# Two fused transformer layers in split fp32: weight slots re-laid so that the two SBUF operands of a matmul sit 192 bytes apart modulo 256

## The chip, the cores and the metric

The kernel runs on one core of a Trainium2 chip. The metric is the device time of one execution in microseconds (us); lower is better. Before the change three runs gave a median of 1536.1 us (1534.24 to 1539.58).

## The reference, cut to what matters

Two layers are computed one after the other on 256 tokens with a model width of 2048, all in fp32. What costs time is the product of a small activation matrix with large weight matrices, each weight used once:

```python
# layer 1 (mLSTM + pooling)
h = rmsnorm(x, norm_pre_w)                      # 256 x 2048
q, k, v, o, z, i, f, u, zb, ga, gb = split(h @ w_in)
y_a = sigmoid(o) * mlstm(silu(conv(q,k)), v, i, f) * silu(z)
y_b = (pool(u) @ pool_w) * pool_scale * silu(zb)
merged = sigmoid(ga) * (y_a @ w_proj_mlstm) + sigmoid(gb) * (y_b @ w_proj_pool)
x = x + rmsnorm(merged @ w_out, norm_post_w)
# layer 2 (16 meta tokens in front: 272 tokens), differential + latent attention
h = rmsnorm(concat(meta, x), attn_norm_w)
a_q, a_k, a_v, a_g, b_cq, b_ckv, b_kr, b_g = split(h @ w_in_2)
s = where(rel >= 0, qk_scores, -inf)            # causal mask in both attentions
oA, oB = diff_attention(...), mla_attention(rmsnorm(b_cq) @ w_uq, rmsnorm(b_ckv) @ w_ukv, b_kr)
y = rmsnorm(x + concat(oA * silu(a_g), oB * silu(b_g)) @ w_out_2, final_norm_w)
```

## The kernel before, in words

**Split products.** Every weight product runs as three fp32r matmuls: high part of the weights times high part of the activations, high times low, low times high. The weights come as a stream of 474 slots. A slot is 256 rows of one 512-column block: two chunks of 128 rows (`c` = 0, 1), each 128 partitions x 512 columns of 4 bytes.

**The ring.** SyncE loads slot n into `raw[n % 4]` (512 KB). ScalarE's `split` (L783) copies it to `wh[n % 4]`, rounded to fp32r; VectorE's `split` (L1077) writes the rest to `wl[n % 4]`. Both work LEAD = 3 slots ahead of TensorE and wait for `slots_done` or for each other, so a slot is split while TensorE works on an earlier one. The `wh` and `wl` buffers are 4096 bytes each per partition, one behind the other, and the two chunks of a slot are 2048 bytes apart.

**The matmuls.** `pe_group` issues all of them, in two forms:

- By feature (L298, L300, L302): the weights are the stationary operand, 128 columns of a chunk at a time (LDWEIGHTS), and the activations of the same 128 rows are the moving operand, 256 columns (272 where the meta tokens are included). A chunk gives 4 blocks x 3 = 12 matmuls, a slot 24.
- By token (L288 to L290): the activations are stationary (128 tokens) and the weights move, 512 columns. A slot gives 12 matmuls. Stages V and WO, the group cq, the second half of UKV, and W2.

**The stages**, in order, with their moving or stationary activations: QK (X), V (X, by token), OZ (X, with the mLSTM heads' small matmuls between slots), UZ (X), MG (groups ga and gb on X, pa on Y, pb on Z), WO (by token), then layer 2: CKQ, AK, AV, AQ on X2, UQ and UKV on the latent activations, G on X2 with attention's small matmuls between slots, W2 (by token).

**Where the operands lie.** In X, Y, Z and the latents `cqh`, `cql` a 128-row chunk of activations is 1024 bytes per partition and starts at a multiple of 256 from the common base. X2 (`x2h`, `x2l`) has 272 columns, so its chunk kc starts 1088*kc bytes in, which is 64*kc modulo 256; where a stage takes the 256 real tokens alone (AQ, G, cq) it starts another 64 bytes later. The weights' blocks start at multiples of 256 bytes everywhere, because 512 columns, 128 columns and the slot are all multiples of 256 bytes. Below, the offset of a matmul is the address of its moving operand less that of its stationary operand, modulo 256, both in bytes within a partition. Before the change it is 0 in all matmuls by feature on X, Y, Z and the latents. In AQ and G it is 64*(kc+1) modulo 256: chunks 0, 4, 8, 12 have 64, chunks 1, 5, 9, 13 have 128, chunks 2, 6, 10, 14 have 192 and chunks 3, 7, 11, 15 have 0. In AK and AV it is 64*kc.

**The mask.** In the attention quarters of G, VectorE adds `cmask` (0 or -1e30) to the latent attention's scores (L1286). The other attention uses `rel` (key position less query position, or -1e30 where masked). Both tables, 416 columns each, are part of `const`, loaded once at the start.

## Time and profile before

| | us |
|---|---|
| median of three runs | 1536.1 |
| the profiled execution, its own time | 1533.42 |
| its span, first to last instruction | 1531.6 |
| TensorE matmul busy (with modelled ends) | 1489.3 |
| TensorE weight load busy | 1407.8 |
| VectorE busy | 839.1 |
| ScalarE busy | 711.0 |
| mean granted TensorE clock | 0.994 |

The records of matmuls overlap: each shows 0.28 us although the next starts 0.12 us later. The pace is therefore read from the start of one to the start of the next, or from the number of instructions in a long window, and never from the mean duration.

### The profile page before, as it was taken

The page shows a single profiled execution, that of the slowest core. Times are in us where ns is not written, and L with a number is a line of the kernel's source. Part 1 is how long each engine was busy: PE and PEld are TensorE (multiplying, and loading weights), DVE is VectorE, ACT ScalarE, POOL GpSimd, SP SyncE. Part 2 cuts the span into 40 slices and gives each one's busy share as a digit, 9 for nine tenths or more (in the row PEclk, how much of TensorE's full clock was granted, in tenths as well). Part 3 has the DMA queues.
Part 4 walks back from the last instruction along what each step waited for, and adds up shares of the span by engine and source line. Part 5 has one row for each costly group of instructions (what it writes and reads, how often), then busy time and mean ns, then how long its engine had stood idle before and what let it go on. Part 6 is the DMA issues. An engine that isn't in the chain of part 4 may idle for free.

```text
span 1531.6 us, 27814 instructions
## 1 busy us (share of the span) xinstructions
PE 1489.3 (97%) x10848; PEld 1407.8 (92%) x10848; DVE 839.1 (55%) x1032; ACT 711.0 (46%) x931; POOL 65.8 (4%) x90
## 2 busy tenths in 40 slices
PE   6999999999999999999999999979999999999997
PEld 6999998899999999999999998868999997888886
DVE  5667664546646555545454544556444444556754
ACT  5454445445455433334333434445433344666542
POOL 0000000101000000000000000000000001111000
PEclk9999999999999999999999999999999999999999
DMA  7565555654455556666566566646655553333563
GB/s 266 168 203 170 177 175 179 196 162 155 160 151 184 173 164 169 186 183 180 178 187 183 176 192 231 212 124 225 202 158 173 166 157 106 102 105 111 195 215 126
DMA packets 70647, 265.01 MB, mean 173 GB/s; under 512 B 7841, under 2 KB 7841, under 8 KB 69281
## 3 DMA queue, kind: packets, MB, share of 16 engines
q1 hardware_dynamic: 69552, 254.45, 53.9%
q0 software_dynamic: 1024, 9.57, 1.7%
q8 instruction: 51, 0.84, 0.2%
q14 instruction: 20, 0.16, 0.0%
HBM read 259.79 MB, written 4.19 MB: 172 GB/s over the span
## 4 chain that ended last, share of the span: by engine, by line
PE 93%; DVE 2%; ACT 2%; DMA 1%; issue 1%; DVEq 0%; POOL 0%; ACTq 0%; SPq 0%; POOLq 0%
PE ps L298 23%; PE ps L302 23%; PE ps L300 23%; PE ps L288 5%; PE ps L289 5%; PE ps L290 5%; PE ps L397 2%; DMA metan<-in_meta 1%; PE ps L635 1%; PE ps L469 1%; PE ps L477 1%; PE ps L642 1%; DVE wl L1077 1%; DMA xn<-in_x 0%; PE ps L640 0%
## 5 line engine op out<-in xcount | busy, mean ns | idle before, releaser
L1077 DVE TENSOR_TENSOR wl<-raw,wh 128x1024 fp32r<-128x1024 f32 x474 | 580.0, 1227 | 570.1 <-ACT wh L783 562.5
L783 ACT ACTIVATE wh<-raw 128x1024 fp32r<-128x1024 f32 x474 | 499.0, 1059 | 563.5 <-PE ps L302 440.5
L298 PE MATMUL ps<-xh,wh 128*128 128x256 f32 x1792 | 510.9, 285 | 1.8 <-DVE xl L1091 1.8
L302 PE MATMUL ps<-xh,wl 128*128 128x256 f32 x1792 | 507.7, 283 | 0.0
L300 PE MATMUL ps<-xl,wh 128*128 128x256 f32 x1792 | 507.6, 283 | 0.0
L298 PEld LDWEIGHTS ps<-xh,wh 128*128 128x128 f32 x1792 | 344.4, 192 | 2.3 <-DVE xl L1091 2.0
L300 PEld LDWEIGHTS ps<-xl,wh 128*128 128x128 f32 x1792 | 344.5, 192 | 0.3
L302 PEld LDWEIGHTS ps<-xh,wl 128*128 128x128 f32 x1792 | 344.5, 192 | 0.0
L298 PE MATMUL ps<-x2h,wh 128*128 128x256 f32 (+1 forms) x688 | 198.8, 289 | 3.5 <-ACTq L896 3.3
L302 PE MATMUL ps<-x2h,wl 128*128 128x256 f32 (+1 forms) x688 | 195.2, 284 | 0.0
L300 PE MATMUL ps<-x2l,wh 128*128 128x256 f32 (+1 forms) x688 | 195.1, 284 | 0.0
L298 PEld LDWEIGHTS ps<-x2h,wh 128*128 128x128 f32 x688 | 129.6, 188 | 7.8 <-issue 6.9
L300 PEld LDWEIGHTS ps<-x2l,wh 128*128 128x128 f32 x688 | 129.7, 188 | 0.1
L302 PEld LDWEIGHTS ps<-x2h,wl 128*128 128x128 f32 x688 | 129.4, 188 | 0.0
L298 PE MATMUL ps<-yh,wh 128*128 128x256 f32 x256 | 72.4, 283 | 0.0
L300 PE MATMUL ps<-yl,wh 128*128 128x256 f32 x256 | 72.4, 283 | 0.0
L302 PE MATMUL ps<-yh,wl 128*128 128x256 f32 x256 | 72.4, 283 | 0.0
L1120 DVE SCALAR_TENSOR_TENSOR work<-ps,small,work 128x255 f32<-128x255 f32 (+2 forms) x96 | 39.5, 475 | 23.6 <-ACT work L824 23.5
L288 PE MATMUL ps<-wh,mh 128*128 128x512 f32 x128 | 50.0, 391 | 2.4 <-DVE wl L1077 2.4
L288 PE MATMUL ps<-wh,oh 128*128 128x512 f32 x128 | 50.3, 393 | 1.8 <-DVE ol L1390 1.8
L289 PE MATMUL ps<-wl,oh 128*128 128x512 f32 x128 | 49.8, 389 | 0.0
L290 PE MATMUL ps<-wh,ol 128*128 128x512 f32 x128 | 49.8, 389 | 0.0
(321 smaller groups left out, 1781.1 us busy)
## 6 DMA issues: line engine op xcount, KB each, us to landing
raw<-in_w_stream SPq DMA_DIRECT2D x474, 512.0 KB, 3.7
xn<-in_x SPq DMA_DIRECT2D x2, 1024.0 KB, 6.1
xr<-in_x POOLq DMA_DIRECT2D x1, 2048.0 KB, 15.1
x_kept<-xr POOLq DMA_DIRECT2D x1, 2048.0 KB, 9.8
x1r<-x_kept POOLq DMA_DIRECT2D x1, 2048.0 KB, 10.4
out<-yn SPq DMA_DIRECT2D x4, 512.0 KB, 2.7
const<-in_const SPq DMA_DIRECT2D x1, 1044.0 KB, 12.5
poolw<-in_pool_w POOLq DMA_DIRECT2D x1, 1024.0 KB, 5.4
```

What stands on the lines that cost most here:

```text
L288: pe.matmul(o, hi[:, kc, t], wh[r][:, c, 0:cols], start=a, stop=False)
L289: pe.matmul(o, hi[:, kc, t], wl[r][:, c, 0:cols], start=False, stop=False)
L290: last = pe.matmul(o, lo[:, kc, t], wh[r][:, c, 0:cols], start=False, stop=z)
L298: pe.matmul(out_at(j), wh[r][:, c, f], hi[:, kc, tokens], start=st, stop=False, skip_group_check=True)
L300: pe.matmul(out_at(j), wh[r][:, c, f], lo[:, kc, tokens], start=False, stop=False, skip_group_check=True)
L302: last = pe.matmul(out_at(j), wl[r][:, c, f], hi[:, kc, tokens], start=False, stop=z, skip_group_check=True)
L397: return pe.transpose(o, i, ident[0:n, 0:n])
L469: last = pe.matmul(ps[:, 5, st * S:st * S + w], kst[:, dt, st * P:(st + 1) * P], qk[:, bass.ds(h * 2 + dt, 1), st * P:S].rearrange("p o s ...
L477: last = pe.matmul(ps[:, 6 + t, 0:VW], lhs, vn[:, st, bass.ds(h * VW, VW)], start=st == 0, stop=st == t)
L783: act.activation(wh[r][:, :, :], raw[r][:, :, :], ACT.Copy).then_inc(wh_done, 1)
L1077: tt(wl[r][:, :, :], raw[r][:, :, :], wh[r][:, :, :].bitcast(F32), ALU.subtract).then_inc(split_done, 1)
L1120: last = stt(out=work[0][:, jj, sh:S], in0=banks(j)[:, jj, 0:S - sh], scalar=small[:, bass.ds(SMALL["conv_w"][0] + q * 16 + 4 * jj + 3 - s ...
```

## The change

The slots `wh` and `wl` grow from 4096 to 4352 bytes (1088 columns), a multiple of 256, and inside a slot the first chunk's start and the distance between the two chunks depend on what the slot is used for. `slot_view` gives the two chunks; the two splits write through it and `pe_group` reads through it.

| layout | first column | pitch | for | offset after |
|---|---|---|---|---|
| BY_FEATURE | 16 (64 bytes) | 512 | all by-feature groups on X, Y, Z, latents | 192 |
| BY_TOKEN | 0 | 512 | v, wo, uv, w2 | 0, as before |
| SECOND | 0 | 528 | aq, g | 64 in even slots, 192 in odd slots |
| SECOND_KEYS | 16 | 528 | cq, ckv, ak, av | by feature 192 in even slots, 64 in odd; cq 0 and 128 |

The last column is worked out from the addresses: a slot's two chunks are kc = 2k and 2k+1, X2 moves on by 64 bytes per chunk, and so does a slot with a pitch of 528 columns; what is left changes by 128 from slot to slot. The first three slots of V and of WO keep the layout of the stage before.

The buffers behind the ring move up by 2048 bytes, a multiple of 256. To make room, `cmask` goes from `const` (1044 KB to 836 KB), and the masked scores come from `rel`: `min(rel + 1e29, scores)`, one SCALAR_TENSOR_TENSOR in place of one TENSOR_TENSOR of the same 416 columns.

No instruction is added, removed or moved on any engine. Some of the splits become 128 x 2 x 512 in place of 128 x 1024.

```diff
+SLOT_W = 1088
+BY_FEATURE, BY_TOKEN, SECOND, SECOND_KEYS = (16, 512), (0, 512), (0, 528), (16, 528)
+LAYOUT_OF = {"v": BY_TOKEN, "wo": BY_TOKEN, "uv": BY_TOKEN, "w2": BY_TOKEN, "cq": SECOND_KEYS, "ckv": SECOND_KEYS,
+             "ak": SECOND_KEYS, "av": SECOND_KEYS, "aq": SECOND, "g": SECOND}
+def slot_layouts():
+    out = []
+    for name, kinds, times in STAGES:
+        of = [LAYOUT_OF.get(kind, BY_FEATURE) for kind in kinds for _ in range(slots_of(kind))] * times
+        if name in ("V", "WO"):
+            of[:LEAD] = out[-LEAD:]
+        out += of
+    return out
-    ("ones", 128), ("dmask", 384), ("inv", 64), ("rel", KEYS), ("cmask", KEYS),
+    ("ones", 128), ("dmask", 384), ("inv", 64), ("rel", KEYS),
-    R_X, R_C, R_Y, R_Z, R_V, R_T = 49152, 83968, 116736, 149504, 165888, 182336
+    R_X, R_C, R_Y, R_Z, R_V, R_T = 51200, 86016, 118784, 151552, 167936, 184384
-    wh = [sb(f"wh{r}", [P, SLOT_KC, COLS], F32R, (RING + r) * KB4) for r in range(RING)]
-    wl = [sb(f"wl{r}", [P, SLOT_KC, COLS], F32R, (2 * RING + r) * KB4) for r in range(RING)]
+    wh_at = [sb(f"wh{r}", [P, SLOT_W], F32R, RING * KB4 + r * 4 * SLOT_W) for r in range(RING)]
+    wl_at = [sb(f"wl{r}", [P, SLOT_W], F32R, RING * KB4 + (RING + r) * 4 * SLOT_W) for r in range(RING)]
+    def slot_view(slot, layout):
+        first, pitch = layout
+        return slot[:, first:first + SLOT_KC * pitch].rearrange("p (c n) -> p c n", n=pitch)[:, :, 0:COLS]
...
-                        pe.matmul(out_at(j), wh[r][:, c, f], hi[:, kc, tokens], start=st, stop=False,
+                        pe.matmul(out_at(j), whr[:, c, f], hi[:, kc, tokens], start=st, stop=False,
...
-            act.activation(wh[r][:, :, :], raw[r][:, :, :], ACT.Copy).then_inc(wh_done, 1)
+            act.activation(slot_view(wh_at[r], layout), raw[r][:, :, :], ACT.Copy).then_inc(wh_done, 1)
...
-                    tt(pm[odd][:, :], ps[:, 4, 0:KEYS], cn("cmask"), ALU.add)
+                    stt(out=pm[odd][:, :], in0=cn("rel"), scalar=1e29, in1=ps[:, 4, 0:KEYS], op0=ALU.add,
+                        op1=ALU.min)
```

## Rows read from the trace of the kernel before

**Rows 1.** The page: busy shares, and the chain that ended last.
```profile
PE 1489.3 (97%) x10848; PEld 1407.8 (92%) x10848; DVE 839.1 (55%) x1032; ACT 711.0 (46%) x931; POOL 65.8 (4%) x90
...
PE 93%; DVE 2%; ACT 2%; DMA 1%; issue 1%; DVEq 0%; POOL 0%; ACTq 0%; SPq 0%; POOLq 0%
```

**Rows 2.** Stretch 620:900 (MG), line L298 alone: busy and count.
```profile
620.00:900.00 280.00, 220.09 (x779) 149.34 (x778) 1.00 0.61 182
```

**Rows 3.** Timeline, AQ's second group, chunks 8 to 11 (start us, us).
```profile
1221.70 0.28 PE L298 MATMUL ps<-x2h,wh 128*128 128x256 f32 x1
...
1223.12 0.28 PE L298 MATMUL ps<-x2h,wh 128*128 128x256 f32 x1
...
1224.55 0.28 PE L298 MATMUL ps<-x2h,wh 128*128 128x256 f32 x1
...
1225.14 0.28 PE L302 MATMUL ps<-x2h,wl 128*128 128x256 f32 x1
...
1225.82 0.28 PE L302 MATMUL ps<-x2h,wl 128*128 128x256 f32 x1
1225.93 0.28 PE L298 MATMUL ps<-x2h,wh 128*128 128x256 f32 x1
...
1226.87 0.28 PE L302 MATMUL ps<-x2h,wl 128*128 128x256 f32 x1
...
1227.35 0.28 PE L298 MATMUL ps<-x2h,wh 128*128 128x256 f32 x1
```

**Rows 4.** Timeline, G's third group, chunk 6: entered after attention's matmuls.
```profile
1368.11 0.28 PE L300 MATMUL ps<-x2l,wh 128*128 128x256 f32 x1
...
1369.28 0.28 PE L302 MATMUL ps<-x2h,wl 128*128 128x256 f32 x1
```

**Rows 5.** Timeline, cq (by token on X2): two rows nine matmuls apart.
```profile
1043.75 0.39 PE L289 MATMUL ps<-wl,x2h 128*128 128x512 f32 x1
...
1045.82 0.39 PE L289 MATMUL ps<-wl,x2h 128*128 128x512 f32 x1
```

**Rows 6.** Stretch 214:254.8 (V, 15 slots), line L288 alone: busy and count.
```profile
214.00:254.80 40.80, 23.34 (x60) 11.26 (x60) 1.00 0.62 182
```

**Rows 7.** Lines by shape: busy us, mean ns, idle before and what ended it.
```profile
L298 PE MATMUL ps<-xh,wh 128*128 128x256 f32 x1792 | 510.9, 285 | 1.8 <-DVE xl L1091 1.8
...
L783 ACT ACTIVATE wh<-raw 128x1024 fp32r<-128x1024 f32 x474 | 499.0, 1059 | 563.5 <-PE ps L302 440.5 <-PE ps L290 108.6 <-issue 9.6
...
L1077 DVE TENSOR_TENSOR wl<-raw,wh 128x1024 fp32r<-128x1024 f32 x474 | 580.0, 1227 | 570.1 <-ACT wh L783 562.5 <-issue 4.0
...
L1253 DVE SCALAR_TENSOR_TENSOR sbd<-const,ps 128x416 f32<-128x416 f32 x16 | 9.7, 645 | 19.9 <-PE ps L635 19.9
...
L1286 DVE TENSOR_TENSOR pm<-ps,const 128x416 f32<-128x416 f32 x8 | 4.7, 584 | 0.0
```

**Rows 8.** Timeline, AK's second group: the starts of chunks 8, 10, 11, 12.
```profile
1120.44 0.28 PE L298 MATMUL ps<-x2h,wh 128*128 128x272 f32 x1
...
1123.46 0.29 PE L298 MATMUL ps<-x2h,wh 128*128 128x272 f32 x1
...
1124.98 0.28 PE L298 MATMUL ps<-x2h,wh 128*128 128x272 f32 x1
...
1126.46 0.28 PE L298 MATMUL ps<-x2h,wh 128*128 128x272 f32 x1
```

**Rows 9.** VectorE's lines in stretch 71.4:117.4 (QK, 16 slots).
```profile
L1077 DVE TENSOR_TENSOR wl<-raw,wh 128x1024 fp32r<-128x1024 f32 x17 | 20.7, 1225 | 8.8 <-ACT wh L783 7.7 <-issue 0.9
L1120 DVE SCALAR_TENSOR_TENSOR work<-ps,small,work 128x254 f32<-128x254 f32 (+2 forms) x24 | 9.9, 474 | 6.1 <-ACT work L824 6.1
L1130 DVE TENSOR_TENSOR qk<-work,work 128x1024 f32 x2 | 2.4, 1220 | 0.0
```

**Rows 10.** Timeline, OZ's first head: `pt` made and taken.
```profile
304.31 0.55 DVE L1435 SCALAR_TENSOR_TENSOR pt<-ps,dmat 128x384 f32<-128x384 f32 x1
...
307.57 1.47 PE L477 MATMUL ps<-vn,pt 128*128 x6
```

More of the change, by code:

```diff
@@ L69 @@
 GATE_W = 32 + H
+SLOT_W = 1088
[10 more added lines that the diff above has]
+    return out
+LAYOUTS = slot_layouts()
 OUT_ORDER = (0, 2, 1, 3)
@@ L254, in pe_group @@
     def pe_group(pe, n, frees, out_at, moving, tiles, tokens, ring=0, kcs=KC, cols=COLS, before=None,
-                 chunk=lambda kc: kc, first_tile_early=False):
+                 chunk=lambda kc: kc, first_tile_early=False, like=None):
         hi, lo = moving
@@ L271, in pe_group @@
             r = (ring + k) % RING
+            layout = LAYOUTS[(n if like is None else like) + k]
+            whr, wlr = slot_view(wh_at[r], layout), slot_view(wl_at[r], layout)
             def free(c, at):
@@ L287, in pe_group @@
                         free(c, m)
-                        pe.matmul(o, hi[:, kc, t], wh[r][:, c, 0:cols], start=a, stop=False)
-                        pe.matmul(o, hi[:, kc, t], wl[r][:, c, 0:cols], start=False, stop=False)
-                        last = pe.matmul(o, lo[:, kc, t], wh[r][:, c, 0:cols], start=False, stop=z)
+                        pe.matmul(o, hi[:, kc, t], whr[:, c, 0:cols], start=a, stop=False)
+                        pe.matmul(o, hi[:, kc, t], wlr[:, c, 0:cols], start=False, stop=False)
+                        last = pe.matmul(o, lo[:, kc, t], whr[:, c, 0:cols], start=False, stop=z)
                 else:
@@ L297, in pe_group @@
                         free(c, j)
-                        pe.matmul(out_at(j), wh[r][:, c, f], hi[:, kc, tokens], start=st, stop=False,
+                        pe.matmul(out_at(j), whr[:, c, f], hi[:, kc, tokens], start=st, stop=False,
                                   skip_group_check=True)
-                        pe.matmul(out_at(j), wh[r][:, c, f], lo[:, kc, tokens], start=False, stop=False,
+                        pe.matmul(out_at(j), whr[:, c, f], lo[:, kc, tokens], start=False, stop=False,
                                   skip_group_check=True)
-                        last = pe.matmul(out_at(j), wl[r][:, c, f], hi[:, kc, tokens], start=False, stop=z,
+                        last = pe.matmul(out_at(j), wlr[:, c, f], hi[:, kc, tokens], start=False, stop=z,
                                          skip_group_check=True)
@@ L418, in groups @@
             in_loop = not isinstance(i, int)
+            one = 1 if in_loop else i
             for j, kind in enumerate(kinds):
@@ L424, in groups @@
                          [slice(m * P, (m + 1) * P) for m in range(TOK)] if by_token else None, slice(0, S),
-                         kcs=slots_of(kind) * SLOT_KC,
+                         kcs=slots_of(kind) * SLOT_KC, like=FIRST[name] + one * per + off,
                          first_tile_early=name == "WO" and not in_loop and (i, j) == (1, 1), before=before and (lambda k, j=j, kind=kind: before(j, kind, k)))
@@ L753, in body @@
                         if not isinstance(i, int) or here + k + LEAD < end:
-                            split(here + k + LEAD, (n0 + off + k + LEAD) % RING)
+                            like = n0 + (i if isinstance(i, int) else 1) * per + off + k + LEAD
+                            split(here + k + LEAD, (n0 + off + k + LEAD) % RING, LAYOUTS[like])
                         if late:
@@ L788, in _ @@
             act.activation(xsq[:, m, :], xn[:, m, :], ACT.Square, accum_out=stat[:, m:m + 1]).then_inc(s_x_squares, 1)
-        split(0, 0)
+        split(0, 0, LAYOUTS[0])
         def high_parts(hi, b, name, s):
@@ L802, in _ @@
             if b + 1 < LEAD:
-                split(b + 1, b + 1)
+                split(b + 1, b + 1, LAYOUTS[b + 1])
         def out_squares(q, m):
@@ L1040, in between @@
             act.drain().then_inc(s_out_squares, 1)
-            split(n, n % RING)
-            split(n + 1, (n + 1) % RING)
+            split(n, n % RING, LAYOUTS[n])
+            split(n + 1, (n + 1) % RING, LAYOUTS[n + 1])
             x1_squares(2)
             x1_squares(3)
-            split(n + 2, (n + 2) % RING)
+            split(n + 2, (n + 2) % RING, LAYOUTS[n + 2])
             for b in range(4):
@@ L1084, in _ @@
                 ts(xn[:, m, q], xn[:, m, q], stat[:, 2 + m:3 + m], None, ALU.mult).then_inc(s_x_normed, 1)
-        split(0, 0)
+        split(0, 0, LAYOUTS[0])
         def low_parts(lo, hi, b, name, s):
@@ L1098, in _ @@
             if b + 1 < LEAD:
-                split(b + 1, b + 1)
+                split(b + 1, b + 1, LAYOUTS[b + 1])
         def split_high_low(hi, lo, src, s):
@@ L1498, in between @@
             x1_rows(1)
-            split(n, n % RING)
+            split(n, n % RING, LAYOUTS[n])
             x1_scale(1)
-            split(n + 1, (n + 1) % RING)
-            split(n + 2, (n + 2) % RING)
+            split(n + 1, (n + 1) % RING, LAYOUTS[n + 1])
+            split(n + 2, (n + 2) % RING, LAYOUTS[n + 2])
             dve.tensor_copy(x2h[:, :, 0:META], metat[:, :, :])
@@ L1695, in const_array @@
     rel = np.where(kpos <= pos, kpos - pos, far)
-    mask = np.where(kpos <= pos, 0.0, far)
     put("rel", np.concatenate([rel[:P, :K0], rel[P:, :]], 1))
-    put("cmask", np.concatenate([mask[:P, :K0], mask[P:, :]], 1))
     slopes = np.exp2(-np.arange(1, 9, dtype=np.float32)) * 8.0
```

9 lines of the change are left out of this document (5 added, 4 removed).

## The prediction

> **What bounds the kernel.** I read the busy shares first: TensorE is busy 97% of the span, and the chain that ended last is TensorE for 93% of it [rows 1]. ScalarE and VectorE are at 46% and 55%, and each waits: ScalarE's split stood idle for 563.5 us in total, 549.1 of it ended by TensorE's matmuls, and VectorE's waited for ScalarE's [rows 7]. So weights are not late; TensorE's own pace sets the time, and what counts is the time from one matmul's start to the next.
>
> The second view is the count of matmuls in a long quiet stretch. In 280 us of MG there are 779 records of L298 [rows 2], which takes every third place; one hangs over the window's left edge, so 280 us / (3 x 778) = 120.0 ns each, with the clock granted in full. At 2.4 GHz, the upper level, 256 columns alone would be 106.7 ns, so 13.3 ns, or 32 cycles, of each are something else. All of these have offset 0.
>
> The third view is the timeline of AQ, because there the same form of matmul, 256 moving columns and 128 x 128 weights, runs at four offsets in turn. Its rows begin at 1221.70, where the ninth chunk (kc = 8) starts. From chunk start to chunk start, 12 matmuls each [rows 3]:
>
> - kc = 8, offset 64: 1.42 us, 118.3 ns each
> - kc = 9, offset 128: 1.43 us, 119.2 ns
> - kc = 10, offset 192: 1.38 us, 115.0 ns
> - kc = 11, offset 0: 1.42 us, 118.3 ns
>
> The first few of a chunk are a passage from the offset before. Inside chunk 10, from 1225.14 to 1225.82, six matmuls take 0.68 us: 113.3 ns each [rows 3], or 272 cycles against the 288 of offset 0. That is the pattern that the change can give to most of the kernel. The last four of chunk 11, back at offset 0, take 0.48 us: 120.0 each, X's own pace. But 113.3 is not the only pattern at offset 192. Chunk 6 of G's third group, also at 192, was entered after attention's matmuls; its second matmul starts at 1368.11 and its twelfth at 1369.28 [rows 4], ten steps in 1.17 us, 117 ns each to within the timeline's rounding of 1 ns; I use 117.8, where chunk 8's 118.3, passage and all, also points. So there are two patterns at 192, and which one a run falls into hangs on how it is entered. I went through all 24 chunks of AQ and G at this offset in the timeline: 16 settle at 113.3, 8 stay near 117.8 to their end. Of the 7 chunks entered straight from the chunk before, 6 settle at 113.3; of the 17 entered after other work, 10. None changes pattern once it has settled, and none is slower than 120.
>
> Is it the relation of the two addresses, or the moving operand's own address? In V and in cq the moving operand is the same `wh` and `wl` at the same addresses, and only the stationary side moves. V gives 60 records of one line in three over 40.8 us, 226.7 ns each [rows 6]; in cq nine steps take 2.07 us, 230.0 ns each [rows 5]. The stationary side matters too, so own address alone is refuted; the relation is the simpler reading.
>
> The Trainium skill speaks against the change: "TensorE: Matmul & The Clock Gate", Part 2, says that the weight load reads through a port of its own and takes no SBUF bandwidth from the running matmul, and its "Back-to-back issue gap" gives N/2.4 + 2.5 = 109.2 ns for 256 columns. By that every offset would run alike and the change be worth nothing; were 109.2 reached instead, an estimate from that page is 72 us of gain. The trace agrees with neither: 113.3 and 120.0 stand in one program for the same form.
>
> **The change part by part.**
>
> *By-feature matmuls on X, Y, Z and the latents.* They go from offset 0 to 192. They are the slots of QK 64, OZ 64, UZ 32, MG 112 and UQ 6: 278 x 24 = 6672, of which 1792 x 3 on X [rows 7]. The first slot ran in the start's half-clock time and some fifty steps hold a wait or other work, so 6630 steps count. At 113.3 in place of 120.0 each saves 6.67 ns, 44.2 us in all; at 117.8 it saves 2.2 ns, 14.6 us. These are the two ends. They divide by runs without a break: QK (64 slots, one run after the start) is worth 10.0 or 3.3 us; from the last pooling matmul of UZ through MG (113 slots, 2700 steps) 18.0 or 6.0; the rest of UZ, two runs, 5.1 or 1.7; OZ (64 slots), broken 24 times by the heads' matmuls, 10.2 or 3.4, and with 10 of 17 such entries in the fast pattern about 7.5; UQ 1.0 or 0.3. I take the fast pattern for the long runs, since the straight entries favour it and long sections let a passage settle: 10.0 + 18.0 + 5.1 + 7.5 + 0.8 = 41.4 us.
>
> *AQ and G, 48 slots, 1152 matmuls.* Only the odd slots get 192, the even ones stay at 64. Before, the four offsets average (118.3 + 119.2 + 115.0 + 118.3)/4 = 117.7. After, half stays at 117.8 and half comes to between 113.3 and 117.8, with two thirds fast 114.8. Gain 576 x 2.9 = 1.7 us, less 0.1. I take 1.6.
>
> *AK, AV and ckv, 32 x 24 + 16 x 9 = 912 matmuls of 272 columns.* Chunks 8 and 9 (offsets 0 and 64) take 3.02 us together, chunk 10 (128) 1.52 and chunk 11 (192) 1.48 [rows 8], so 125.8, 125.8, 126.7, 123.3 ns. Half at 192 and half at 64 afterwards is 124.6 on average against 125.4: 0.7 us.
>
> *By token.* V, WO, uv and W2 keep offset 0. Three slots each of V and WO, 72 matmuls, get offset 64; by cq's 230.0 that is 72 x 3.3 = 0.2 us lost. cq itself, 96 matmuls, has half at 0 afterwards: 48 x 3.3 = 0.2 won. Nil together, and within 0.7 either way.
>
> *The splits.* The same columns, some as two pieces of 512. Neither row shows such a shape; nearest are 1059 ns and 1227 ns themselves [rows 7]. I take no change, and bound it by none and by a tenth more, 0.23 us per slot for the pair. Both are hidden while TensorE takes 2.72 us per slot: V already runs there, 12 x 226.7 ns, without a break over 15 slots [rows 6]. The tightest place is QK, where VectorE also does the convolution: 20.7 + 9.9 + 2.4 = 33.0 us in 46 [rows 9], 72%; TensorE at 113.3 ns does these 16 slots in 43.5 us, and VectorE is at 76%. VectorE still idles 8.8 + 6.1 us there. The group's burst of convolution work, four or five slots long, loses at most 5 x 0.16 = 0.8 us of its lead. I take 0, up to 1 us lost.
>
> *The heads.* TensorE reaches `pt` at 307.57, 2.7 us after VectorE made it (304.31 + 0.55) [rows 10]. Three or four slots between question and answer shrink by 0.16 us each, 0.64 at most. No new wait.
>
> *The mask.* TENSOR_TENSOR of 416 columns is 584 ns, a SCALAR_TENSOR_TENSOR with the same table and PSUM is 645 [rows 7]: 8 x 61 ns = 0.5 us on VectorE, beside TensorE's slot work. 0. The shorter `const` is loaded behind the first four slots and nothing waits for it: 0.
>
> Sum: 41.4 + 1.6 + 0.7 + 0 = 43.7 us, less 0.7 for small waits and the rounding of entries: 43. The profiled execution's 1533.4 becomes 1490.4 (its span 1531.6 to 1488.6). The median of the runs lies 2.7 us above the profiled one, so the forecast in its terms is 1493.
>
> **The rivals.**
>
> A. *One of the long runs locks into the slow pattern.* For: 8 of 24 chunks did, mostly those entered after other work, and both long runs begin so. Against: straight entries settled fast. Price: MG's run 18.0 - 6.0 = 12 us, 1505; QK's 6.7 us, 1500; both 1512; every run slow is 14.6 + 1 or so of gain, 1520.
>
> B. *The address relation is not what sets the pace of X.* AQ and G differ from X in the operands' region and pitch too, and weight load and moving operand may not meet there at all; the other 13.3 ns would be a fixed cost. Then nothing changes but the small terms: 1534 to 1537. For: only X2's chunks show 113.3. Against: offset-0 chunks of X2 run at X's 120.0 once settled [rows 3], and V against cq.
>
> C. *Slower: at a fixed offset of 192 X settles in a third, worse pattern.* For: taking the stationary side off offset 0 did make cq slower, by 3.3 ns a matmul [rows 5, 6]. If each of the 6630 steps lost the same 3.3 ns to the 120.0, they would cost 22 us: 1558. It decides as soon as the settled step is above 120.0 ns. Against: no chunk at 192 shows it, 24 of them.
>
> **How the numbers follow.** Main case 1493 (1487 to 1498): 0.52. Rival A, 1498 to 1521: 0.31. B: 0.09. C: 0.05. A gain over 49 us, if a long run finds a pattern still faster than any seen: 0.03. The range of 1487 to 1519 holds the main case and nearly all of A, 0.82; the main case's own range is 1487 to 1498. A change under 0.3%, 4.6 us, can't be told from none. Faster: 0.52 + 0.31 + 0.03 = 0.86, and a little of B goes either way, 0.01 of it faster; same 0.07; slower 0.06.
>
> **What would show it.** Right: 280 us of MG hold some 824 records of L298 in place of 779; the timeline in MG steps by 0.11 and 0.12 us, 0.34 for three; V and W2 still 12 matmuls in 2.72 us; ScalarE's split still released by TensorE, with less idle. A shows as steps of 117.8 ns through all of MG or QK; OZ may show both between heads. B shows 120.0 in MG with 113.3 still in G's odd slots. New waits of TensorE for `wl` in QK would show the cover gone. The forecast is wrong if the settled step on X is neither 113.3 nor 117.8 ns.

## The result, and the profile after

The changed kernel takes 1517.8 us (median of 4 runs, 1516.8 to 1520.2) against 1535.3 for the kernel before (1534.2 to 1539.6): ratio 0.988, 95% interval 0.986 to 0.991. That is 17.4 us of gain where 43 were forecast. The time lies inside the range, and beside the figure of rival A for "every run slow", 1520. The profiled execution took 1517.3, its span 1515.5.

The page of the changed kernel, its busy shares, its chain, and the costliest lines (line, engine, operation, count, busy us and mean ns, idle before and what ended it). By-feature matmuls are now L323, L325 and L327.

```profile
PE 1471.6 (97%) x10848; PEld 1389.7 (92%) x10848; DVE 839.0 (55%) x1032; ACT 711.2 (47%) x931; POOL 66.5 (4%) x90
...
PE 93%; DVE 2%; ACT 2%; DMA 2%; issue 1%; DVEq 0%; POOL 0%; ACTq 0%; SPq 0%; POOLq 0%
...
L1104 DVE TENSOR_TENSOR wl<-raw,wh 128x1024 fp32r<-128x1024 f32 x474 | 579.9, 1227 | 555.5 <-ACT wh L810 547.8
L810 ACT ACTIVATE wh<-raw 128x1024 fp32r<-128x1024 f32 x474 | 499.3, 1059 | 545.7 <-PE ps L327 422.4
L323 PE MATMUL ps<-xh,wh 128*128 128x256 f32 x1792 | 506.6, 283 | 2.3 <-DVE xl L1119 2.3
```

What bounds the kernel is what bounded it before [rows 1]: TensorE is busy 97%, and only its total shrank, 1489.3 to 1471.6. The splits take 1227 and 1059 ns as before [rows 7], and TensorE waits for no new thing. The idle of ScalarE's split fell from 563.5 to 545.7 us, about what TensorE's total lost.

Line L323 alone in two quiet stretches, QK and MG: length, busy and count of matmuls and of weight loads, granted clock, DMA share, GB/s.

```profile
30.00:190.00 160.00, 127.24 (x453) 84.96 (x454) 1.00 0.60 187
620.00:900.00 280.00, 222.71 (x793) 148.72 (x793) 1.00 0.62 186
```

The second row answers to [rows 2], the records of L298 in the same stretch before: 793 records in place of 779, where the forecast wanted 824. 280 / (3 x 792) = 117.8 ns a step; QK's 160 / (3 x 452) = 118.0 says the same to the rounding of a count. The timeline, one slot of MG, rows nine steps apart (start us, us):

```profile
699.85 0.28 PE L323 MATMUL ps<-xh,wh 128*128 128x256 f32 x1
...
700.91 0.28 PE L323 MATMUL ps<-xh,wh 128*128 128x256 f32 x1
```

1.06 us over nine steps is 117.8. In OZ both patterns stand in one stage. First eight steps of a slot from before a head's work, then nine of one behind it:

```profile
298.29 0.28 PE L325 MATMUL ps<-xl,wh 128*128 128x256 f32 x1
...
299.20 0.28 PE L323 MATMUL ps<-xh,wh 128*128 128x256 f32 x1
...
307.85 0.28 PE L325 MATMUL ps<-xl,wh 128*128 128x256 f32 x1
...
308.91 0.28 PE L325 MATMUL ps<-xl,wh 128*128 128x256 f32 x1
```

0.91 / 8 = 114 ns, within the timeline's rounding of 113.3; 1.06 / 9 = 117.8. Stage by stage, from the first matmul of a stage to the first of the next (W2 to the end of the span), with the mean step, from one matmul's start to the next one's, over all steps without other work or a wait between. "In the fast pattern" are slots that settle at 113.3 ns:

| stage | us before | after | gain | step before | after | slots in the fast pattern |
|---|---|---|---|---|---|---|
| QK | 192.4 | 189.0 | 3.4 | 120.0 | 117.8 | 0 of 64 |
| OZ | 213.0 | 208.6 | 4.3 | 119.9 | 117.0 | 13 of 64 |
| UZ | 99.1 | 95.9 | 3.2 | 120.0 | 115.8 | 14 of 32 |
| MG | 322.6 | 316.6 | 6.0 | 120.0 | 117.8 | 0 of 112 |
| WO | 106.3 | 108.8 | -2.5 | 226.9 | 227.1 | |
| AQ, G | 205.2 | 203.9 | 1.3 | 117.7 | 116.5 | mixed |
| V, ckv/cq, AK, AV, UQ, UKV, W2 | 376.1 | 375.6 | 0.5 | | | |

The sum is 16.2 us; the spans differ by 16.1, since the first matmul comes 0.1 us later. UZ is fast until the first pooling matmul and slow to its end, and MG stays so for 2700 steps.

WO lost what nobody had forecast. The chain of the changed kernel in WO (start, us, what):

```profile
918.56 16.19 DMA metan<-in_meta
...
936.93 1.06 ACT wh L810
938.02 1.24 DVE wl L1104
939.39 0.77 PE ps L313
```

The load of the meta tokens takes 16.2 us (15.2 before) and holds ScalarE and VectorE up; their split is late and TensorE waits 3.3 us (before 2.4). Two stretches behind that wait (PE, weight loads, VectorE, ScalarE, GpSimd, then the granted clock, DMA share, GB/s; the first still holds the last 0.3 us of the wait):

```profile
939.10:942.50 3.40, 3.11 (x7) 2.49 (x8) 3.40 (x5) 1.74 (x2) 1.98 (x1) 0.51 0.52 152
942.60:946.00 3.40, 3.40 (x17) 2.77 (x16) 0.10 (x1) 1.83 (x5) 0.54 (x1) 1.00 0.94 324
```

The clock is granted at 0.51, the lower of its two levels, 1.2 of 2.4 GHz, for 3.4 us: 7 matmuls in place of 17 in the next such stretch. Before had no such stretch in WO. Whether the change did this is asked below.

### The profile page after: what moved, and what is told of

It is laid out like the page before. It is cut to its first block, busy times and chain, and to the rows that moved or that the text cites. A ratio compares the mean times of both kernels' runs of the same rounds, so it can differ in the third digit from the quotient of the medians.

```text
span 1515.5 us, 27814 instructions
## 1 busy us (share of the span) xinstructions
PE 1471.6 (97%) x10848; PEld 1389.7 (92%) x10848; DVE 839.0 (55%) x1032; ACT 711.2 (47%) x931; POOL 66.5 (4%) x90
## 4 chain that ended last, share of the span: by engine, by line
PE 93%; DVE 2%; ACT 2%; DMA 2%; issue 1%; DVEq 0%; POOL 0%; ACTq 0%; SPq 0%; POOLq 0%
PE ps L323 23%; PE ps L327 23%; PE ps L325 23%; PE ps L313 6%; PE ps L314 5%; PE ps L315 5%; PE ps L422 2%; DMA metan<-in_meta 1%; PE ps L661 1%; PE ps L495 1%; PE ps L503 1%; PE ps L668 1%; DVE wl L1104 1%; DMA xn<-in_x 0%; PE ps L666 0%
## 5 line engine op out<-in xcount | busy, mean ns | idle before, releaser
L1104 DVE TENSOR_TENSOR wl<-raw,wh 128x1024 fp32r<-128x1024 f32 x474 | 579.9, 1227 | 555.5 <-ACT wh L810 547.8
L810 ACT ACTIVATE wh<-raw 128x1024 fp32r<-128x1024 f32 x474 | 499.3, 1059 | 545.7 <-PE ps L327 422.4
L323 PE MATMUL ps<-xh,wh 128*128 128x256 f32 x1792 | 506.6, 283 | 2.3 <-DVE xl L1119 2.3
L327 PE MATMUL ps<-xh,wl 128*128 128x256 f32 x1792 | 503.3, 281 | 0.0
L325 PE MATMUL ps<-xl,wh 128*128 128x256 f32 x1792 | 503.2, 281 | 0.0
L327 PEld LDWEIGHTS ps<-xh,wl 128*128 128x128 f32 x1792 | 342.0, 191 | 0.0
L323 PEld LDWEIGHTS ps<-xh,wh 128*128 128x128 f32 x1792 | 338.7, 189 | 2.8 <-DVE xl L1119 2.5
L325 PEld LDWEIGHTS ps<-xl,wh 128*128 128x128 f32 x1792 | 337.6, 188 | 0.3
L323 PE MATMUL ps<-x2h,wh 128*128 128x256 f32 (+1 forms) x688 | 198.4, 288 | 3.5 <-ACTq L923 3.3
L327 PE MATMUL ps<-x2h,wl 128*128 128x256 f32 (+1 forms) x688 | 194.8, 283 | 0.0
L325 PE MATMUL ps<-x2l,wh 128*128 128x256 f32 (+1 forms) x688 | 194.4, 283 | 0.0
L323 PEld LDWEIGHTS ps<-x2h,wh 128*128 128x128 f32 x688 | 129.3, 188 | 7.8 <-issue 6.9
L325 PEld LDWEIGHTS ps<-x2l,wh 128*128 128x128 f32 x688 | 129.8, 189 | 0.1
L327 PEld LDWEIGHTS ps<-x2h,wl 128*128 128x128 f32 x688 | 129.2, 188 | 0.0
L323 PE MATMUL ps<-yh,wh 128*128 128x256 f32 x256 | 71.9, 281 | 0.0
L325 PE MATMUL ps<-yl,wh 128*128 128x256 f32 x256 | 71.9, 281 | 0.0
L327 PE MATMUL ps<-yh,wl 128*128 128x256 f32 x256 | 71.9, 281 | 0.0
L314 PE MATMUL ps<-wl,mh 128*128 128x512 f32 x128 | 50.4, 394 | 0.0
L315 PE MATMUL ps<-wh,ml 128*128 128x512 f32 x128 | 50.3, 393 | 0.0
## 6 DMA issues: line engine op xcount, KB each, us to landing
xr<-in_x POOLq DMA_DIRECT2D x1, 2048.0 KB, 16.1
```

What stands on the lines that cost most here:

```text
L314: pe.matmul(o, hi[:, kc, t], wlr[:, c, 0:cols], start=False, stop=False)
L315: last = pe.matmul(o, lo[:, kc, t], whr[:, c, 0:cols], start=False, stop=z)
L323: pe.matmul(out_at(j), whr[:, c, f], hi[:, kc, tokens], start=st, stop=False, skip_group_check=True)
L325: pe.matmul(out_at(j), whr[:, c, f], lo[:, kc, tokens], start=False, stop=False, skip_group_check=True)
L327: last = pe.matmul(out_at(j), wlr[:, c, f], hi[:, kc, tokens], start=False, stop=z, skip_group_check=True)
L810: act.activation(slot_view(wh_at[r], layout), raw[r][:, :, :], ACT.Copy).then_inc(wh_done, 1)
```

## The experiments

All edit the changed kernel. But for the four executions at the end, which leave it as it is, they replace its table of layouts by a function of stage, iteration, group, kind and slot that gives first column and pitch; first columns are in 4-byte words, so on X (16, 512) is offset 192 and (48, 512) offset 64. "Fast" and "slow" are the settled steps of 113.3 and 117.8 ns. A starter is a slot put at another offset in order to change the pattern of the slots behind it.

### All slots at the old offset

```diff
+def layout_at(name, i, j, kind, k):
+    return BY_TOKEN
```

> All slots in the layout of before (first column 0, pitch 512) inside the wider slots, with the moved buffers and the derived mask kept. Theory (only the offset of the two operands matters): the pace of every stage returns to before's, 120.0 ns on X, 117.5 to 117.9 in AQ and G, and the time to 1535 us, within 2. Rival (the wider slots, the moved regions or the shorter constant block give part of the 17 us): some of the 2.2 ns on X stays and the time is below 1530.

1535.6 us, ratio 1.001 (0.9996 to 1.002). All matmuls of TensorE in a stretch of QK and one of MG:

```profile
30.00:190.00 160.00, 160.00 (x1336) 1.00 0.59 183
620.00:890.00 270.00, 270.00 (x2252) 1.00 0.60 183
```

160 / 1335 and 270 / 2251 are 119.9 ns; from start to start QK's step is 119.99 ns, MG's 120.00, G's 117.84. The wider slots, the moved regions and the derived mask stay and are worth nothing that shows (the interval allows 0.6 us of gain and 3.4 of loss), as the prediction's zeros had it; the gain is the offset's. TensorE waits 3.3 us in WO here too, and the clock falls for 3.4 us behind it: WO's loss doesn't need the new offset.

### X moved in place of the weights

```diff
-    return LAYOUT_OF.get(kind, BY_FEATURE)
+    return (48, 512) if name == "V" else BY_TOKEN
-    xh = sb("xh", [P, KC, S], F32R, R_X)
+    xh = sb("xh", [P, KC, S], F32R, R_X + 192)
```

(`xl` likewise; Y, Z and the latents stay at offset 0.)

> Every weight slot by feature in the layout of before, and X itself moved up by 192 bytes, so that the moving operand changes its address and the stationary one does not; Y and Z stay. V's slots move up by 192 too, to keep offset 0 (its first three are left at 64). Theory (the relation of the two addresses sets the pace): QK, OZ, UZ and the groups ga and gb of MG run at 117.8 or 113.3 ns, pa and pb at 120.0. Rival (the weights' own start address, 64 bytes past a multiple of 256, is what helped): all stay at 120.0.

1503.3 us, one execution. All matmuls of TensorE in three stretches (the count is the number in brackets): first QK, then a group of MG on X and the next one, on Y.

```profile
30.00:190.00 160.00, 160.00 (x1414) 1.00 0.62 193
...
590.00:610.00 20.00, 20.00 (x179) 1.00 0.63 194
612.50:632.50 20.00, 20.00 (x169) 1.00 0.62 187
```

160 / 1413 = 113.2 ns in QK. On X 20 / 178 = 112 ns, on Y 20 / 168 = 119, both to the count's rounding; step by step, 113.3 and 120.0. The weights never left offset 0, so it is the relation of the two addresses that counts: rival B is refuted from the other side too. And the long run of QK fell into the fast pattern here, at the same offset of 192 at which it was slow in the changed kernel. OZ has 39 fast slots of 64 where the changed kernel has 13. So the offset gives the two paces and not which of them is caught. QK's fast pattern need not come from the move: this execution had no low clock at its start, which the last experiment takes up.

### Single slots at another offset

```diff
+PRIMED = {("QK", 0, 3): 32, ("QK", 1, 3): 48, ("MG", 0, 3): 0, ("MG", 1, 3): 24, ("MG", 2, 3): 32, ("MG", 3, 1): 48}
+    if (name, j, k) in PRIMED:
+        return PRIMED[name, j, k], 512
```

> The changed kernel, with single slots of another offset put into the long runs, each followed by slots at 192: in QK the fourth slot of each group (offset 128 in the first of a pair, 64 in the second), in MG the fourth slot of ga (0), pa (160), gb (128) and the second of pb (64). Theory (two stable patterns at 192, chosen at entry; QK and MG happened to fall into the slow one): behind some of these slots the run goes on at 113.3 ns, as it did behind offsets 128 and 64 in AQ and G, and stays there until the next such slot; with half of the slots fast, 12 to 16 us are gained, 1503. Rival (QK and MG can't run faster than 117.8 for a reason of their own, such as the distance of the buffers): every slot at 192 in QK and MG stays at 117.8 and the time stays at 1518.

1506.1 us, ratio 0.983 (0.981 to 0.985). QK stayed slow behind its first slot at offset 128. Behind its first slot at 64 it was fast to its end, the later slots at other offsets aside: matmuls that were fast ahead of a slot at 128 were so again behind it, all seven times, three in QK and four in MG. MG's `ga` was slow behind each slot at 0 and fast behind each slot of `pa` at 160, four times of four. The timeline at such a hand-over; the slot at 160 begins at 626.18, the slot back at 192 at 628.99.

```profile
625.47 0.28 PE L335 MATMUL ps<-yh,wh 128*128 128x256 f32 x1
...
626.18 0.28 PE L335 MATMUL ps<-yh,wh 128*128 128x256 f32 x1
...
628.99 0.28 PE L335 MATMUL ps<-yh,wh 128*128 128x256 f32 x1
...
629.33 0.28 PE L335 MATMUL ps<-yh,wh 128*128 128x256 f32 x1
...
629.67 0.28 PE L335 MATMUL ps<-yh,wh 128*128 128x256 f32 x1
```

Six steps in 0.71 us (118), then three in 0.34 and three in 0.34 (113.3). Nothing waits here: one group, the same offset before and behind, two patterns, and a slot at another offset between them.

### A map of offsets

```diff
+OF_KIND = {("QK", 0): 8, ("QK", 1): 24, ("OZ", 0): 4, ("OZ", 1): 12, ("UZ", 0): 20, ("UZ", 1): 28,
+           ("MG", 0): 32, ("MG", 1): 48, ("MG", 2): 40, ("MG", 3): 56}
```

> The changed kernel with one other offset per kind of group, to read the pace at each: by feature on X, Y, Z 224 and 160 in QK, 240 and 208 in OZ, 176 and 144 in UZ, 128, 64, 96 and 32 in MG; by token 128, 192, 32, 224 in V, 0, 64, 96, 160 in WO and 0, 16, 48, 240 in W2. Theory (the pace hangs on the offset in steps of 64 bytes, and 192 has a fast and a slow pattern): offsets not a multiple of 64 lie between their neighbours, none is below 113.3 ns, and by token none is below 226.7. Rival (the fast pattern at 192 is the edge of a better place): some offset between 128 and 256 runs at 113.3 or less in every slot of its kind. The time itself says little, 1515 to 1560.

1530.1 us, one execution. Settled steps by feature: 0: 120.0 ns (from before), 32: 116.5, 64: 117.8, 96: 120.0, 128: 118.4 to 118.9, 160: the same, 176: 118.1 to 118.9, 208: 117.6, 224: 118.2, 240: 118.3 to 120.0, 144: up to 120.5. By token 0 is best, 226.7; 64 gives 228.5, 16 231.6, and the others 231.9 to 236.8. The changed kernel sits at the best of both, if the fast pattern is caught. That offsets between multiples of 64 lie between their neighbours did not come true: 32 lies below both, 96 and 144 above both. Two of the rows behind it, MG at 96 and at 32:

```profile
656.00:674.00 18.00, 18.00 (x153) 1.00 0.64 191
677.00:688.00 11.00, 11.00 (x97) 1.00 0.57 177
```

A count takes in the two matmuls that began up to 0.28 us before the stretch and hang into it: (18 + 0.28) / 153 = 119.5 ns and (11 + 0.28) / 97 = 116.3, where the steps read 120.0 and 116.5.

### The meta tokens loaded first

```diff
+        pool.dma_start(metan[:, :], meta).then_inc(s_meta, 16)
         pool.dma_start(postw[:, :], post_w).then_inc(s_post, 16)
```

> The changed kernel with the load of the meta tokens issued before the two larger loads on GpSimd's queue. In the changed kernel TensorE waits 3.3 us in WO for a split that stands behind this load, and its granted clock is at the lower level for 3.4 us there, which before did not show. Theory (this wait and the lowered clock behind it took back part of the gain): both go, WO is shorter by about 3.3 + 1.7 = 5 us, 1513. Rival (the clock falls there for another reason, or the wait moves to the next load, of the residual rows): the wait is replaced by one of like length and the time stays within 1 us of 1518.

1508.9 us (1505.7 to 1514.1), ratio 0.984 (0.981 to 0.986). WO falls from 108.8 to 103.7 us; the wait is gone, and with it the low clock there:

```profile
932.00:945.00 13.00, 13.00 (x59) 10.78 (x58) 7.22 (x7) 7.44 (x10) 0.57 (x1) 1.00 0.75 243
```

The profiled execution, 1514.1, gained 3.2 us of these 5.0: at the border of WO and CKQ the low clock lasted 17.1 us in place of 10.2, and CKQ took 1.9 us more. The two quickest runs took 1505.7, 8.4 us less than the profiled one. A fast QK (6.7 us) and a shorter low clock (1.9) would come to about that, but there is no trace of them.

### All of layer 2's queries and gates at 192

```diff
+    if kind in ("aq", "g"):
+        return (0, 528) if k % 2 else (32, 528)
```

> The changed kernel with the even slots of AQ and G moved by 32 columns, so that every chunk of these two stages is at 192 in place of half of them. Theory (a pattern is kept until a step of another offset; at the border of the two chunks of a slot the next weights are fetched while the old chunk still moves, one step at 128, and this ends the fast pattern; only coming from 64 starts it): with no chunk at 64 left, nearly all of AQ runs at 117.8 and the mean is 117.2 to 117.8 ns against 116.5 in the changed kernel, AQ 47.4 us to 47.7 and G up to 0.7 us longer. Rival (more chunks at 192 are simply better): the mean falls to 115.0 to 116.0 and AQ takes 0.4 us less.

1516.9 us, ratio 0.989 (0.987 to 0.991). AQ took 47.5 us against 47.4, G 156.2 against 156.4. AQ's time lies where the theory put it, but G isn't longer, and AQ isn't slow throughout: 45 of the 48 slots of AQ and G run their first chunk fast and their second slow, here one in AQ whose second chunk begins at 1195.60:

```profile
1194.68 0.28 PE L332 MATMUL ps<-x2h,wh 128*128 128x256 f32 x1
...
1195.37 0.28 PE L332 MATMUL ps<-x2h,wh 128*128 128x256 f32 x1
...
1196.07 0.28 PE L332 MATMUL ps<-x2h,wh 128*128 128x256 f32 x1
...
1196.78 0.28 PE L332 MATMUL ps<-x2h,wh 128*128 128x256 f32 x1
```

Six steps in 0.69 us (115, its last one 117), and six in 0.71 (118). This was the odd finding that led to the rule tested below.

### Starters at 64, without and with the meta tokens first

```diff
+PRIMED = {("QK", 0, 0, 2), ("UQ", 0, 0, 0), ("UZ", 0, 1, 6), ("UZ", 1, 1, 6),
+          ("OZ", 0, 0, 3), ("OZ", 1, 0, 3), ("OZ", 0, 1, 0), ("OZ", 1, 1, 0), ("OZ", 0, 1, 3), ("OZ", 1, 1, 3)}
+    return (48, 512) if (name, i, j, k) in PRIMED else LAYOUT_OF.get(kind, BY_FEATURE)
```

> The changed kernel with one slot at offset 64 (first column 48) at the head of each unbroken run: QK's third slot alone, in OZ the fourth of o and the first and fourth of z, the seventh of each zb in UZ, the first of UQ. Theory (the slot starts the fast pattern and nothing ends it before the next break): QK behind it, 16 slots of UZ, all 112 of MG and 5 of UQ at 113.3, 11 of 16 slots of each OZ round; 6.6 + 1.6 + 12.0 + 0.5 + 3.3 = 24 us less than the changed kernel's 1517.8, so 1494, ratio to before 0.973. Rival (the pattern decays over long runs or needs a new start at each loop turn): MG slips back to 117.8 and the time is above 1500.

> The kernel of the run before with the meta tokens loaded ahead of the two larger loads. Theory (the wait in WO is behind this load, and the two gains add): 3 to 5 us less than that kernel, 1490, ratio to before 0.970. Rival (TensorE, faster, reaches the residual rows' load before it lands and waits at the end of WO instead): no more than 1 us of difference.

1509.6 us, ratio 0.984 (0.982 to 0.986), and with the meta tokens first 1503.3, ratio 0.980 (0.979 to 0.981). QK was fast from its fourth slot on, UQ in 5 of 6 slots, OZ 32 of 64. But UZ's starters failed, and MG stayed slow for all its 316.6 us: the absolute forecasts missed by its 12 us and UZ's 1.6. Behind 10 of the 16 starters at 64 the next slot was fast. Between their profiled executions WO gives 4.5 us and CKQ, whose low clock was shorter in the second, 1.8; the start and QK take 1.2 back.

### Starters at 160

```diff
+PRIMED = {("QK", 0, 0, 2): 48, ("UQ", 0, 0, 0): 48}
+STARTERS = {("UZ", 1, 6), ("MG", 0, 3), ("OZ", 0, 3), ("OZ", 1, 0), ("OZ", 1, 3)}
+    return (24, 512) if (name, j, k) in STARTERS else LAYOUT_OF.get(kind, BY_FEATURE)
```

(The meta tokens are loaded first here too.)

> As the last kernel, but the slots that head a run in UZ (seventh of zb), MG (fourth of each ga) and OZ are at offset 160 in place of 64 (QK's third and UQ's first stay at 64, which worked). Theory (a slot at 64 settles at 117.8 itself and hands over at any point of that pattern, so it starts the fast one only sometimes, while 160 took MG from slow to fast 4 times of 4): all of MG from the fourth slot on at 113.3, 12 us less than the last kernel, 1491. Rival (which pattern follows hangs on chance in the hand-over and 160 is no better than 64): MG stays at 117.8 for at least one of its four rounds, 1494 to 1503.

**1490.2 us** (1488.7 to 1492.3), ratio 0.970 (0.967 to 0.973): it beats both kernels, the changed one by 1.8% (0.9704 / 0.9883), meta load included. The forecast was 1491. QK and MG, all matmuls:

```profile
30.00:190.00 160.00, 160.00 (x1415) 1.00 0.62 195
620.00:890.00 270.00, 270.00 (x2381) 1.00 0.65 192
```

270 / 2380 = 113.4 ns in MG, which takes 305.3 us: 108 slots fast and 4 starters at 120.0. UZ has 30 of 32 slots fast, OZ 31 of 64. QK was fast here from its second slot, ahead of its starter, so that starter is not shown to have done anything here. MG's first starter and what follows:

```profile
598.75 0.28 PE L338 MATMUL ps<-xl,wh 128*128 128x256 f32 x1
...
601.15 0.28 PE L336 MATMUL ps<-xh,wh 128*128 128x256 f32 x1
...
601.50 0.28 PE L336 MATMUL ps<-xh,wh 128*128 128x256 f32 x1
...
601.84 0.28 PE L336 MATMUL ps<-xh,wh 128*128 128x256 f32 x1
```

Twenty steps in 2.40 us (120.0), then three in 0.34. Starters at 160 led to the fast pattern 14 times of 18, and in all 6 cases where the starter's own slot had settled at 120.0.

### X moved, the rest as in the changed kernel

```diff
+ON_X = ("qk", "o", "z", "u", "zb", "ga", "gb")
+    if name == "V":
+        return 48, 512
+    return BY_TOKEN if kind in ON_X else (48, 512) if (kind, j, k) == ("uq", 0, 0) else LAYOUT_OF.get(kind, BY_FEATURE)
```

(X moved as above, and the meta tokens first.)

> X moved up by 192 bytes with its weight slots at 0, as in e5, and in addition the slots of pa, pb, the latents and layer 2 as in the changed kernel, and the meta tokens loaded first. No starter slots except UQ's first. Theory (only the offset and the hand-over count): QK fast from the start as in e5; pa and pb leave 120.0 for 113.3 or 117.8; 1503 less 7.7 or 2.6 for pa and pb, 1.6 for AQ and G, 0.9 for UQ, 3 to 5 for the meta load: 1488 to 1495. Rival (in e5 it was the groups at offset 0 between them that started ga and gb afresh each time): ga and gb now run at 117.8 too, and the time is 1500 or more.

1497.9 us (1494.9 to 1503.6), ratio 0.977 (0.974 to 0.980). QK is fast in all slots, and MG's 64 slots on X; its 48 on Y and Z are slow, so MG takes 309.9 us. One kernel thus has both patterns at 192 side by side, group by group. The profiled execution, 1494.9, lies in the theory's range, the median above it. Where `pa` ends and `gb` begins, at 632.84:

```profile
632.13 0.28 PE L335 MATMUL ps<-yh,wh 128*128 128x256 f32 x1
...
632.84 0.29 PE L335 MATMUL ps<-xh,wh 128*128 128x256 f32 x1
...
634.21 0.28 PE L335 MATMUL ps<-xh,wh 128*128 128x256 f32 x1
...
634.89 0.28 PE L335 MATMUL ps<-xh,wh 128*128 128x256 f32 x1
```

Six steps in 0.71 us (118), a passage of a few steps, and in the next chunk six in 0.68 (113.3). Nothing waits, and no slot stands at another offset. But X and its weights have other addresses than Y, Z and theirs, so the one step across such a border has an offset of its own: 0 from Y or Z to X, 128 from X to Y or Z. All 7 borders at 0 turned slow to fast, all 8 at 128 fast to slow.

### All of layer 2's queries and gates at 64

The odd finding above led me to read AQ and G again by the single step at each chunk border, in which the next chunk's weights are loaded while the last chunk's moving operand is read, so that this step has an offset of its own.

```diff
+    if kind in ("aq", "g"):
+        return (32, 528) if k % 2 else (0, 528)
```

> The changed kernel with AQ's and G's chunks placed so that each has offset 64 (even slots first column 0, odd slots first column 32, pitch 528). Read again with an eye on the one step at a chunk border, where the next chunk's weights are loaded while the last chunk's moving operand is read, the traces so far give this rule. Border step at offset 0: the pattern is kept, 31 of 31 borders without other work (changed kernel). Border step at 128: fast turns to slow 64 of 64 times, slow to fast 20 of 29 times (changed kernel and the one with all chunks at 192). Here every border step is at 0. The rule: each chunk keeps the pattern of the chunk before, in AQ and G, until other work breaks in; so both chunks of a slot are alike, where the changed kernel had 19 fast first chunks turn slow. AQ's first three slots stay fast (113.4) throughout, since the first is fast at the same entry in the changed kernel. Rival (the pattern is lost or found by chance or by the chunk's own offset): mixed pairs remain, or all is 117.8, as a lone look at QK's slot at 64 would have it. The time is not what this is for: entries after other work at 64 were fast in 4 of 16 slots of G, so G 156.8 us (155.5 to 157.3) against 156.4, AQ 46.3 to 47.9 against 47.4; whole kernel 1518, within 2.

1514.4 us (2 runs), ratio 0.988 (0.983 to 0.994). All borders without other work have their step at 0 here, and the pattern was kept in 62 of 62: 8 times fast, 54 times slow. AQ's first three slots stayed fast and all thirteen behind the first break slow. That the first was fast was luck: with the changed kernel's layouts in AQ the first three were fast in seven executions and slow in five. G's second slot, its second chunk beginning at 1258.33:

```profile
1257.31 0.28 PE L332 MATMUL ps<-x2h,wh 128*128 128x256 f32 x1
...
1257.99 0.28 PE L332 MATMUL ps<-x2h,wh 128*128 128x256 f32 x1
...
1258.67 0.28 PE L332 MATMUL ps<-x2h,wh 128*128 128x256 f32 x1
...
1259.36 0.28 PE L332 MATMUL ps<-x2h,wh 128*128 128x256 f32 x1
```

0.68, 0.68 and 0.69 us per six steps: 113.3 to 115 across the border, at offset 64, where the map alone had shown 117.8. In the changed kernel the same slot, at 192, with a border step at 128:

```profile
1263.87 0.28 PE L323 MATMUL ps<-x2h,wh 128*128 128x256 f32 x1
...
1264.55 0.28 PE L323 MATMUL ps<-x2h,wh 128*128 128x256 f32 x1
...
1265.25 0.28 PE L323 MATMUL ps<-x2h,wh 128*128 128x256 f32 x1
...
1265.95 0.28 PE L323 MATMUL ps<-x2h,wh 128*128 128x256 f32 x1
```

0.68, then 0.70 and 0.70: fast before the border, slow behind it. The rule in AQ and G, over three kernels: a border step at 0 keeps the pattern (31 of 31, and 62 of 62 foretold); one at 128 turns fast to slow (64 of 64) and slow to fast (20 of 29). Outside AQ and G it holds only in part. The kernel before this one has both steps at its group borders in MG: the one at 128 turned fast to slow as here, 8 of 8, but the one at 0 turned slow to fast, 7 of 7. Its chunks behind the border are at 192, those behind a border step at 0 in AQ and G are at 64, and another group and operand begin there; no run separates the two. That the border's own step counts shows elsewhere too: in the first kernel with X moved all 7 borders at 0 led from 120.0 to the fast pattern, while the slots at 0 among the single slots, left by a step at 192, led to the slow one 4 times of 4. What I hadn't expected was QK: with the changed kernel's layouts it ran fast in this execution.

### The changed kernel, four more executions

No edit; the question is whether QK's pattern belongs to the code or to the execution.

> The changed kernel as it is, a second look. In the kernel with AQ's and G's chunks at 64, whose code up to there is that of the changed kernel, QK ran at 113.3 in 63 of its 64 slots, where the changed kernel had 117.8 (6.7 us). Theory: QK's first slot falls into the stretch of low clock of the start, which ended at 20.9 us in the one and 21.5 in the other, so the pattern that QK is left in differs from execution to execution: among four looks at the changed kernel some show QK at 117.8 and some at 113.3, with the span then 6 to 7 us shorter; all behind QK stays as it was (OZ 13 fast slots, MG all at 117.8). Rival: the placing of AQ's chunks, which sets the addresses of nothing in QK, changed it all the same: then all four looks show 117.8 in QK.

> As the look before it: the same kernel, QK at 117.8 or 113.3 by the theory, at 117.8 alone by the rival.

> As the look before it: the same kernel, QK at 117.8 or 113.3 by the theory, at 117.8 alone by the rival.

> As the look before it: the same kernel, QK at 117.8 or 113.3 by the theory, at 117.8 alone by the rival.

1512.1, 1513.7, 1517.3 and 1514.5 us. TensorE's matmuls in QK and MG in the first execution:

```profile
30.00:190.00 160.00, 160.00 (x1414) 1.00 0.62 195
620.00:890.00 270.00, 270.00 (x2295) 1.00 0.62 187
```

The second, QK:

```profile
30.00:190.00 160.00, 160.00 (x1360) 1.00 0.60 187
```

160 / 1413 = 113.2 against 160 / 1359 = 117.7: the first has QK fast, the three others slow. So QK's pattern belongs to the execution. Over all eight profiled executions of kernels with these layouts in QK it was fast in two. MG was slow in all eight, with the same 13 fast slots in OZ and 14 in UZ each time, although the clock's low stretches lay elsewhere. AQ differs too: its first three slots are slow in the first of the four and fast in the others, and G has 7 fast slots in the first and 5 in the others.

In most executions QK's first slot falls into the start's low clock. Where that stretch lay does not settle the pattern: from 18.1 to 21.5 us QK was fast and from 18.3 slow, and from 16.4, 17.5 and 17.6 slow. But whether there was one goes with it. Three executions with QK at 192 had none, the first of these four and the two with X moved, and all three were fast from the first or the second slot on. Of the eleven that had one, two were fast before any starter stood. So few are no proof, and nothing here sets the start's clock by itself.

WO in these four: the wait for the split was 3.7, 1.8, 2.1 and 1.8 us, and low clock followed it for 6.8 us, not at all, 3.4 and not at all. One stretch of all engines in the third:

```profile
938.00:941.40 3.40, 3.40 (x10) 2.63 (x9) 2.90 (x4) 1.03 (x2) 2.62 (x1) 0.50 0.71 213
```

The same stretch in the second:

```profile
938.00:941.40 3.40, 3.40 (x16) 2.81 (x16) 2.59 (x4) 1.77 (x4) 2.62 (x1) 1.00 0.89 237
```

10 matmuls at the lower level, 16 at the upper. WO took 110.2, 105.7, 107.7 and 105.8 us, on both sides of before's 106.3: its 2.5 us are within this scatter around one transfer.

## Why the prediction was wrong

- **The mechanism held.** The offset of moving and stationary address sets the pace, both ways of making it gave the same pace, and there are the two patterns read at 192 [rows 3, 4]. At "Back-to-back issue gap" of "TensorE: Matmul & The Clock Gate" the Trainium skill has 109.2 ns for 256 columns, as the gap of an isolated matmul; for a stream with a weight load before each matmul it says that both set the spacing. The prediction took the figure without that condition. No run reached it, 113.3 being the best at any offset. Nor did all offsets run alike, as its Part 2 on the weight load's own port would have it.
- **Each end was right.** QK slow was put at 3.3 us and gave 3.4; MG slow at 6.0 gave 6.0; UZ's rest, 1.7 to 5.1, gave 3.2; UQ 0.3 of 0.3; AQ and G 1.3 of 1.6; AK and AV 0.3 of 0.7. OZ, taken at 7.5, gave 4.3: 13 of 64 slots fast, where 10 of 17 entries were assumed.
- **The step that failed** is "I take the fast pattern for the long runs, since the straight entries favour it and long sections let a passage settle". MG's run was slow in all eight executions (12 us), QK's in six of them (6.7 us, the profiled one among them). With OZ's 3.2 and UZ's 1.9 that is 23.8 of the 26.9 us by which the profiled span missed its forecast, 1515.5 for 1488.6; WO's 2.5 is most of the rest.
- **Why it failed.** Both halves of its reason fall. A pattern, once held, doesn't settle into the better one: MG kept the slow one for 2700 steps. It changed only where a step or a slot had another offset: behind starters at 160 (316.6 to 305.3 us), and at the group borders when X alone was moved. And the seven straight entries of the old trace weren't straight: each came from a chunk at offset 128, with a border step at 128, and six of them turned fast, just as the slow pattern turned into the fast one at 20 of 29 such borders later. X, Y and Z have no such step between chunks, the addresses recurring modulo 256. The sample held what turns the pattern over; the runs it was applied to did not.
- **Rival A had it**, and its own sentence "mostly those entered after other work, and both long runs begin so" was the better reading: 10 of 17 such entries were fast, which is no case for taking both long runs fast. Its price for both long runs slow was 1512. That 1517.8 lies nearer its 1520, for every run slow, is partly chance: 27 slots of OZ and UZ were fast, and WO's 2.5 us made up for part of them. B and C are refuted.
- **The zeros** for splits, mask, heads and by-token stages were right: 1.001 with all else kept. WO's wait and low clock weren't priced at all; they come and go without any change in the code.

Open: what in the hand-over picks the pattern. In MG, OZ and UZ it is the same each time behind the same code, in QK and AQ it is not. The starters' odds (10 of 16 at 64, 14 of 18 at 160) say that more than the offset counts. Not tried: a layout that turns AQ and G fast by one border step at 128 and then holds it with steps at 0, which the rule there would allow; and one that puts a single step at 0 into a long run at 192, as the borders in MG suggest.

## What to carry to other kernels

Read TensorE's pace from the starts of equal matmuls over a stretch, per moving operand, and ask for both addresses modulo 256 before taking it for granted. A pace can have several stable patterns at one alignment: what a short mixed section shows doesn't carry over to a long uniform one until one knows what switches them, so compare what stands ahead of each sample with what stands ahead of the run. Where a run is locked into the worse one, one slot at another alignment can free it for 0.2 us, and it pays to profile more than one execution. Test a rule found in one stage against every other place where its condition occurs: here one rule held 93 times in two stages and failed 7 times of 7 in a third.

## What the runs showed of the hardware

- One form of matmul (256 columns, 128 x 128 weights, full clock) holds 113.3 or 117.8 ns a step at offset 192 and at 64, for up to 2700 steps. At 0 it is 120.0; no offset beats 113.3 by feature or 226.7 by token (offset 0).
- A single step at offset 128 between two chunks turned fast to slow in 72 of 72 cases (64 in AQ and G, 8 in MG). One at 0 changed nothing in 93 of 93 where the chunk behind it was at 64, and turned slow to fast in 7 of 7 where it was at 192.
- The pattern can differ between executions of one kernel: QK was fast in 2 of 8 (6.7 us), AQ's first three slots in 7 of 12. In MG, OZ and UZ it came out alike each time.
- By feature, TensorE's step was up to 6.7 ns longer or shorter with the relation of its two operands' addresses. "SBUF — State Buffer" of the Trainium skill, under "Who interferes with whom", gives TensorE independent ports for the moving operand and the weight load and says that it never waits on anyone; in these runs moving either operand changed the pace, so the two reads are not independent here.
- Waits of 1.8 to 3.7 us in WO were followed by 3.4 or 6.8 us at the lower clock in some executions and by none in others: none at 1.8 us twice and at before's 2.4, some at 2.1.
